# Cross attention's second values in another PSUM bank, and a new order of work at the last MLP's entry

## The reference

```python
# first block, twice (i = 0, 1)
q = (x @ wq).reshape(B, S, 4, 256)
s = einsum('bshd,bmhd->bhsm', q, mem_k) / 16
p = softmax(s)
o = einsum('bhsm,bmhd->bshd', p, mem_v).reshape(B, S, 1024)      # "values" of four heads
x = layer_norm(ALPHA * x + o @ wo, ...)
...
# second block, once
x = x + g_a * hybrid_mixer(...)            # ends with merged @ w_out
h = rms_norm(x, g_ffn) * (1.0 + sc_f) + sh_f
x = x + g_f * ((silu(h @ w_gate) * (h @ w_up)) @ w_down)         # w_gate, w_up: 1024 x 2816
return rms_norm(x, g_final)
```

## Time and profile before

| | |
|---|---|
| time, median of 3 runs | 941.67 us (941.52 to 941.69) |
| profiled execution | 941.75 us, of which the profile's span is 940.1 us |
| TensorE busy | 931.7 us, 99% of the span |
| VectorE busy | 705.8 us, 75% |
| ScalarE busy | 521.5 us, 55% |
| GpSimd busy | 61.1 us, 7% |
| granted TensorE clock | 0.999 of full speed |

### The profile page before, as it was taken

The page is one execution under the profiler, slowest core; times in us unless marked ns, Lnnn a source line. Parts: engine busy times, 40 slices in busy tenths (PEclk is TensorE's granted clock), DMA queues, the critical chain, the costliest instruction groups (busy, mean ns, idle before and its releaser), DMA issues.

```text
span 940.1 us, 13078 instructions
## 1 busy us (share of the span) xinstructions
PE 931.7 (99%) x5073; PEld 806.2 (86%) x5073; DVE 705.8 (75%) x981; ACT 521.5 (55%) x738; POOL 61.1 (7%) x98
## 2 busy tenths in 40 slices
PE   9999999999999999999999999999999999999997
PEld 8889888988888888889888888888998888888886
DVE  6976678688888776777788877678769886556575
ACT  5757463636655555455275555556566675444543
POOL 0000211001000002100100000002100000000020
PEclk9999999999999999999999999999999999999999
DMA  9695475456988886274399888773633475656521
GB/s 328 239 362 181 135 239 170 174 179 226 336 284 293 285 295 196 102 275 137 127 321 333 285 295 289 246 267 122 233 113 113 135 245 182 222 179 196 173 79 45
DMA packets 109661, 203.00 MB, mean 216 GB/s; under 512 B 4333, under 2 KB 75265, under 8 KB 106273
## 3 DMA queue, kind: packets, MB, share of 16 engines
q1 hardware_dynamic: 106000, 189.15, 59.4%
q0 software_dynamic: 3168, 12.24, 3.8%
q10 hardware_dynamic: 432, 0.79, 0.2%
HBM read 201.09 MB, written 1.06 MB: 215 GB/s over the span
## 4 chain that ended last, share of the span: by engine, by line
PE 95%; DVE 2%; ACT 1%; issue 1%; POOL 0%; POOLq 0%; DVEq 0%; ACTq 0%
PE WB L380 21%; PE WB L386 11%; PE YB L407 11%; PE YB L414 11%; PE YB L422 11%; PE YB L475 6%; PE WB L407 3%; PE WB L414 3%; PE WB L422 3%; PE WB L360 2%; PE WB L367 2%; PE WB L363 2%; PE YB L898 2%; PE WB L513 2%; PE WB L758 1%
## 5 line engine op out<-in xcount | busy, mean ns | idle before, releaser
L1847 DVE TENSOR_TENSOR wl<-raw,wh 128x2048 fp32r<-128x2048 f32 x144 | 331.0, 2306 | 104.8 <-ACT wh L1191 99.9
L1191 ACT CAST wh<-raw 128x2048 fp32r<-128x2048 f32 (+1 forms) x147 | 279.9, 1907 | 36.9 <-PE YB L422 14.8
L380 PE MATMUL WB<-XS,wh 128*128 128x512 f32 x864 | 206.8, 390 | 0.0
L380 PEld LDWEIGHTS WB<-XS,wh 128*128 128x128 f32 x864 | 160.8, 188 | 32.5
L386 PEld LDWEIGHTS WB<-XS,wl 128*128 128x128 f32 x864 | 111.7, 191 | 4.8
L386 PE MATMUL WB<-XS,wl 128*128 128x256 f32 x864 | 113.2, 283 | 0.0
L407 PE MATMUL YB<-wh,FHT 128*128 128x512 f32 x344 | 106.6, 391 | 0.0
L414 PE MATMUL YB<-wl,FHT 128*128 128x512 f32 x344 | 106.2, 390 | 0.0
L422 PE MATMUL YB<-wh,FLT 128*128 128x512 f32 x344 | 106.1, 389 | 0.0
L1381 ACT COPY U<-WB 128x256 f32<-128x256 f32 x102 | 33.1, 376 | 125.4 <-PE WB L386 125.4
L414 PEld LDWEIGHTS YB<-wl,FHT 128*128 128x128 f32 x344 | 64.6, 188 | 13.8
(11 more groups left out here) (386 smaller groups left out, 1261.2 us busy)
## 6 DMA issues: line engine op xcount, KB each, us to landing
raw<-in_mlp_w SPq DMA_DIRECT2D x64, 1024.0 KB, 5.2
raw<-in_w_ada_t SPq DMA_DIRECT2D x24, 1024.0 KB, 4.9
raw<-in_mlstm_w_in SPq DMA_DIRECT2D x11, 1024.0 KB, 8.4
raw<-in_w_ffn_down SPq DMA_DIRECT2D x11, 1024.0 KB, 4.9
raw<-in_w_ffn_gate SPq DMA_DIRECT2D x10, 1024.0 KB, 5.4
raw<-in_w_ffn_up SPq DMA_DIRECT2D x10, 1024.0 KB, 5.6
raw<-in_mem_w_kv SPq DMA_DIRECT2D x8, 1024.0 KB, 8.2
raw<-in_xattn_wq SPq DMA_DIRECT2D x8, 1024.0 KB, 7.0
```

The costliest lines, as they stand in the source:

```text
L380: e.matmul(W[:, :], H[:, at(k, f)], XS[:, k, :], start=k == 0, stop=False)
L1191: f = e.copy(w[:, 0:a * b], raw[:, 0:a * b])
L1847: f = e.tensor_tensor(L[:, 0:a * b], raw[:, 0:a * b], H[:, 0:a * b].bitcast(F32), ALU.subtract)
```

## The change

In cross attention, the values of head 1 go into YB3 instead of a bank from the rotation. They wait for the query's low part of head 1 to have been made out of YB3 (`"ql"`); in the output projection's first chunk, the group for t = 1 and the second half, which writes YB3 too, waits for the low part of head 1's values (`"o"`), and the group for t = 1 and the first half, in YB2, waits as before for the query's low part of head 0.

At the last MLP's entry:

- ScalarE rounds the first gate chunk ahead of the copies of the attention values of heads 2 and 3 instead of behind them.
- VectorE makes the low part of the first up chunk in four pieces (256, 640, 704, 448 columns) instead of three (512, 512, 1024), with other work between them; the third piece raises a semaphore, and TensorE waits for it and, at the last column block, for the whole, in the first t and the second chunk (`up_low`).
- The square of the second half for t = 0 is made by ScalarE, that of the second half for t = 1 by VectorE (before, the other way round); ScalarE's square for (1, 0) comes after the read-outs for t = 0.
- VectorE reads out the transposed block 1 ahead of the gated read-outs for t = 1 instead of between them, and makes the second mean ahead of the first low part instead of behind it.

```diff
@@ pair (TensorE)
+                def up_low(k):
+                    if k == 4:
+                        e.wait_ge(*w_lo0["up"])
+                    elif k == 7:
+                        e.wait_ge(*w_lo[ms[1]])
+
...
                         part(n, t, WH, XH, ln_hi(s, t), start=True)
+                        if s == "ffn" and n == 1 and t == 0:
+                            part(n, t, WL, XH, up_low)
+                            continue
                         e.wait_ge(*w_lo[ms[n]])
@@ xattn (TensorE)
                 def values(h):
-                    W = bank(("xv", i, h))
+                    if h == 1:
+                        e.wait_ge(*dve_xa["ql", i, 1])
+                        W = bank_of["xv", i, h] = YB[3]
+                    else:
+                        W = bank(("xv", i, h))
...
                 def free(t, nb):
-                    return dve_xa["ql", i, nb] if t else act_xa["ct", i, nb]
+                    if t:
+                        return dve_xa["o", i, 1] if nb else dve_xa["ql", i, 0]
+                    return act_xa["ct", i, nb]
@@ scalar
             mla_t(3)
+            hi_to(M["gate", 0])
             mla_v(2)
             mla_v(3)
-            hi_to(M["wout2", 1] + 3)
+            hi_to(M["up", 0])
...
             def ffn_between():
-                ffn_square(1, 1)
+                ffn_square(1, 0)
                 hi_to(M["gate", 1])

             ffn_square(0, 0)
+            ffn_square(0, 1)
             scaled("ffn", 0, 1)
-            norm("ffn", lambda k: MC[:, 32 + k:33 + k], lambda k: MC[:, 24 + k:25 + k], ffn_between,
-                 lambda: ffn_square(1, 0))
+            norm("ffn", lambda k: MC[:, 32 + k:33 + k], lambda k: MC[:, 24 + k:25 + k], ffn_between)
@@ vector
             lo_to(M["gate", 0])
+            lo_part(M["up", 0], 0, 256)
             gated("wout2", dve_mix, 0, 0, 0)
             gated("wout2", dve_mix, 0, 0, 1)
-            rms_square("ffn", 0, 1, dve_mix["gated", 0, 1])
-            rms_mean("ffn", 0, (act_ln["ms", "ffn", 0, 0], dve_ln["ms", "ffn", 0, 1]))
-            lo_part(M["up", 0], 0, 512)
+            lo_part(M["up", 0], 256, 896)
+            rms_mean("ffn", 0, (act_ln["ms", "ffn", 0, 0], act_ln["ms", "ffn", 0, 1]))
             rms_z("ffn", 0, 0)
-            lo_part(M["up", 0], 512, 1024)
+            lo_part(M["up", 0], 896, 1600).then_inc(w_lo0.add("up"))
+            evac("ffn", 0, 1, g, b)
             gated("wout2", dve_mix, 0, 1, 0)
-            evac("ffn", 0, 1, g, b)
             gated("wout2", dve_mix, 0, 1, 1)
-            lo_part(M["up", 0], 1024)
+            lo_part(M["up", 0], 1600)
+            rms_square("ffn", 1, 1, dve_mix["gated", 1, 1])
+            rms_mean("ffn", 1, (act_ln["ms", "ffn", 1, 0], dve_ln["ms", "ffn", 1, 1]))
             rms_low("ffn", 0, 0)
-            rms_mean("ffn", 1, (act_ln["ms", "ffn", 1, 1],))
             rms_low("ffn", 0, 1)
             rms_z("ffn", 1, 0)
```

More of the change, by code:

```diff
@@ L1858, in lo_part @@
                     at[:] = [n + 1, m + 1]
+                return f
             e.memset(XL[:, 7, :].bitcast(F32), 0.0).then_inc(dve_zero.add("x"))
```

## The result

The changed kernel takes 943.24 us (median of 18 runs, 943.05 to 943.91) against 941.70 for the kernel before (18 runs, 941.51 to 942.02): the ratio is 1.0016, its 95% interval 1.001 to 1.0022. So it is 1.5 us slower, 0.16%: a small difference, but the interval lies above 1.

The account below looks back on a forecast made before the run. The prediction took the kernel as a TensorE queue with almost no holes, so any matmul delay is paid in full; +1.92 in cross attention and -0.5 at the entry gave 943.2 us, range 942.2 to 944.0.

Parts of the forecast that it names:

- The bank's gain: Both cross attentions: head 1's values no longer wait for head 2's exponentials; 0.42 us back per stage, -0.84 in all.
- The new wait: First projection chunk: last group waits 1.28 us for head 1's values' low part, plus 0.10 restart; +1.38 per stage.
- The bound that the restart might be free: Uncertainty of the cross-attention part: restarting TensorE after the wait could cost nothing, -0.2 us.
- the rival of the falling clock: Cross attention: the stop drops the clock to 1.2 GHz, both stages lose 2.8 us more, 948.8; chance 0.02.
- The entry: Last MLP's entry: all its edits together sum to -0.54, taken as -0.5 us.
- the root and the scaling: Entry: GpSimd's root takes 0.55 with nothing beside it, scaling ends before TensorE arrives; -0.53 us.
- the steps behind it (-0.24 + 0.30 - 0.07): Entry after the first transposition: block 1 sooner, two new low-part stops, and a small later stop gone.
- Read-out of block 1 first, -0.24: Entry: VectorE reads transposed block 1 ahead of the gated read-outs, so TensorE's first group loses its stop; -0.24 us.
- the 0.25 stays: Entry: TensorE's 0.25 us stop at block 3's rounding on ScalarE remains, since TensorE gains as much as ScalarE.
- The two stops at the low parts, +0.30: Entry: low parts of blocks 0 and 3 each come 0.05 us late, plus 0.10 restart; +0.30 us.
- The rival "taken up later": After cross attention: a later stop independent of TensorE absorbs the delay, leaving about 941.5; chance 0.07.

Follow-up runs that it names:

- e1: Kernel before plus only the bank change (head 1's values in YB3, with the projection's wait on their low part); 943.64 us, ratio 1.002.
- e10: Kernel before plus the YB3 bank change, with VectorE making head 1's values' and head 2's probabilities' low parts ahead of the weight conversion; entry as before; 940.82 us.
- e3: Changed kernel with VectorE making the low part of head 1's values ahead of the 128 x 2048 weight conversion in cross attention; 940.66 us.
- e5: Changed kernel with VectorE making the low parts of head 1's values and head 2's probabilities both ahead of the weight conversion; 940.34 us.
- e2: Changed kernel with the YB3 bank change undone, so only the last MLP's entry differs from the kernel before; 941.28 us, ratio 0.9995.
- e4: Changed kernel with VectorE's 640-column low-part piece behind the first mean instead of ahead, so it runs beside GpSimd's root; 943.61 us.
- e8: Changed kernel with ScalarE again rounding gate 0 behind the copies of the last two heads' values; 943.74 us.
- e7: Changed kernel with VectorE's read-out of block 1 back between the gated read-outs at the last MLP's entry; 943.04 us.
- e9: Changed kernel with both low parts ahead of the weight conversion in cross attention and block 1's read-out between the gated read-outs; 940.17 us, ratio 0.9983.

## Why the prediction was right

The forecast was 943.2, the runs gave 943.24. That they meet within 0.04 is partly luck: the sum worked out was +1.42 on the profiled execution's 941.75, and the runs show +1.54 by the medians and +1.57 by the distance. Step by step:

**The bank's gain**, -0.42 a stage: shown by the start times (no gap at 184.79, 1.60 us; 8.84 us against 9.28 in e1) and by e10, -0.9 for both stages.

**The new wait**, +1.38 a stage: the stop is 1.30 us plus 0.11 to restart, and e1 measures the part at +1.9 with 1.92 forecast. That it comes from VectorE's order and nothing else is shown by e3 and e5, which give back 2.6 and 2.9 us without touching TensorE or a bank; the two waits cost some 0.14 more together than the 2.76 forecast. The bound that the restart might be free is excluded, and so is the rival of the falling clock, with 1.00 over both stops.

**The entry**, -0.5: -0.4 to -0.5 (changed against e1 0.40 by the medians; e2 against before 0.47). The sum is right and its first step, the root and the scaling (-0.53), is shown by e4 and e8 for two of the edits that carry it. The root took 0.56 where 0.55 was forecast. From the last pair of matmuls to the transposition it is 0.45 us instead of 0.92, and the wait before is gone; from the transposition to the next gate chunk it is 14.69 us instead of 14.72. So the whole gain lies ahead of the transposition, and the steps behind it (-0.24 + 0.30 - 0.07) cancel, as their sum says. No run undoes the exchange of the squares or the cut into four pieces by itself; what they give alone is not shown.

**The step that failed** is "Read-out of block 1 first, -0.24" together with "the 0.25 stays". The stop at block 1 did vanish and the one at block 3 did stay, as the trace shows; but the price was counted as if the stops were separate. e7 and e9 show that this edit costs 0.15 to 0.2 us instead of giving 0.24, and the trace of e7 shows the reason: with a stop of 0.31 us at block 1, and without VectorE's wait for the transposed block, three later stops of 0.58 us together shrink to 0.10. The two stops at the low parts, +0.30, came nearly as worked out (0.15 and 0.19). The prediction had what it takes to see this: it counts a wait of 0.24 us of VectorE for the transposed block ahead of the second mean (measured 0.15). Without this edit its own figures put the low part of block 0 at 753.23 - 0.24 = 752.99, wanted at 753.18 + 0.24 = 753.42, so the +0.30 belongs to this edit and not beside it. The total held because I had walked the whole order to the end of the stage; only the share of the single edit was wrong.

**The rival "taken up later"** is excluded by the distance, +1.57 between two points in the trace 580 us apart. The entry's gain differs by 0.15 us between the pairs (0.38 and 0.53 by the distance), but at the transposition it is 0.46 in both (748.40 to 749.31 in e1 and 749.21 to 749.66 in the changed kernel; 0.92 in the kernel before and 0.46 in e2). The rest lies ahead of that point: from head 0's values to the last pair before the transposition the changed kernel takes 567.73 us, e1 and e8 567.63 and e7 567.66. It is most likely scatter; no run settles it.

## What to carry to other kernels

When a buffer is handed to another user, ask who reads it last in the new order, find that instruction in its engine's queue, and add up what stands ahead of it: here a bank gained 0.42 us a stage and cost 1.4, because of one unrelated 2.28 us instruction in front of its last reader. Where the new wait is known, look first whether that instruction can be moved behind: the cheapest fix was a change of order on another engine. And price edits in a stage with several small stops by walking the whole stage, since a stop taken away early can reappear later.

## What the runs showed of the hardware

GpSimd's power of one number per row took 0.55 to 0.56 us by itself, and where an instruction of VectorE with two inputs in SBUF had started before it, it ended 0.41 to 0.42 us after that instruction's end, three times alike: 745.82 + 0.68 against 745.99 + 0.93; 747.75 + 0.81 against 747.92 + 1.06 in e4; and 658.69 + 2.29 against the 658.91 + 2.48 of the earlier trace rows, beside this piece in VectorE's timeline of the kernel before:

```profile
658.69 2.29 DVE L1847 TENSOR_TENSOR wl<-raw,wh 128x2048 fp32r<-128x2048 f32 x1
```

The profiled execution of the changed kernel took 943.91, 0.67 above its own median, and the start explains most of it: its first matmul for the gates waited 0.54 us for ScalarE (the third line of the waits above), and in its trace head 0's values lie 0.57 us later than in that of before. The start of the head-0 values lay between 180.77 (e1) and 181.48 (changed) in the twelve traces, of kernels that do not differ up to there. Without the distance between two inner points I would have read the entry as 0.5 us slower than it is.
